# Gated delta rule: key products made on even steps only, odd steps' matrices built by GpSimd from kept copies

## What is computed

```python
decay = jnp.where(tri, jnp.exp(jnp.where(tri, gc[..., :, None] - gc[..., None, :], 0.0)), 0.0)
kb = k * beta[..., None]
lmat = jnp.where(strict, jnp.einsum('bhncd,bhnsd->bhncs', kb, k) * decay, 0.0)
tmat = lax.linalg.triangular_solve(eye + lmat, eye, left_side=True, lower=True)
a_qk = jnp.einsum('bhncd,bhnsd->bhncs', q, k) * decay
...
def step(s, inp):
    v_new = uu - ww @ s
    o = qd @ s + aa @ v_new
    s = s * jnp.exp(gl)[..., None, None] + jnp.einsum('bhcd,bhce->bhde', kd, v_new)
    return s, o
```

## Time and profile before

| | us |
|---|---|
| median of three runs | 2649.49 |
| lowest, highest | 2646.41, 2654.41 |
| the profiled execution, its time | 2650.06 |
| the profiled execution, its span | 2647.9 |
| the scan's eight rounds within it | 921.33 to 1077.47 |

### The profile page before, as it was taken

One profiled execution on the slowest core, in us unless ns is written; L12 is line 12 of the kernel. 1 busy time (PEld: TensorE's weight loads), 2 busy tenths in 40 slices (PEclk: granted clock), 3 DMA queues, 4 the chain that ended last, 5 costly groups with the idle time before them and its releaser, 6 DMA issues.

```text
span 2647.9 us, 43653 instructions
## 1 busy us (share of the span) xinstructions
PE 2502.6 (95%) x15985; PEld 2049.3 (77%) x15985; DVE 1164.5 (44%) x2120; ACT 752.8 (28%) x1539; POOL 1586.7 (60%) x1567
## 2 busy tenths in 40 slices
PE   6999999999999799999999999878999999989997
PEld 4767788887688699778888757866788887678997
DVE  2384511223469787542122330364422223575455
ACT  2263311111541444231111123252311101363332
POOL 2545577775557222557777555685577775655664
PEclk8999999999999899999999999899999999999999
DMA  7355332244523000333334442103323344502552
GB/s 249 101 171 173 115 109 98 96 159 159 177 65 96 32 2 2 116 123 99 100 101 157 161 162 90 55 1 110 129 96 99 101 156 168 196 28 96 184 176 100
DMA packets 217162, 305.07 MB, mean 115 GB/s; under 512 B 7331, under 2 KB 155550, under 8 KB 217023
## 3 DMA queue, kind: packets, MB, share of 16 engines
q1 hardware_dynamic: 190095, 249.66, 28.6%
q10 hardware_dynamic: 26928, 53.48, 5.7%
HBM read 302.07 MB, written 1.05 MB: 114 GB/s over the span
## 4 chain that ended last, share of the span: by engine, by line
PE 80%; DVE 11%; ACT 2%; POOL 2%; issue 2%; DMA 1%; SPq 1%; DVEq 0%; POOLq 0%; ACTq 0%; PEldq 0%
PE bank L1226 42%; PE bank L1945 12%; PE bank L1277 3%; PE bank L1241 2%; PE bank L1976 2%; PE bank L1724 2%; PE bank L1261 2%; PE bank L1774 1%; PE bank L1768 1%; PE bank L1356 1%; PE bank L1332 1%; DVE ztmp L2214 1%; DVE ast L2141 1%; POOL cqf L726 1%; PE bank L1246 1%
## 5 line engine op out<-in xcount | busy, mean ns | idle before, releaser
L657 POOL TENSOR_TENSOR w_lo<-w_raw,w_hi 128x512 fp32r<-128x512 f32 x652 | 858.2, 1316 | 93.7 <-POOL w_hi L654 72.0
L654 POOL TENSOR_SCALAR w_hi<-w_raw 128x512 fp32r<-128x512 f32 x652 | 429.0, 658 | 616.2 <-PE bank L1226 387.0
L1226 PE MATMUL bank<-u_lo,w_hi 128*128 128x512 f32 (+1 forms) x2048 | 759.2, 371 | 9.0 <-DVE u_lo L2062 5.9
L1226 PE MATMUL bank<-u_hi,w_hi 128*128 128x512 f32 (+1 forms) x2048 | 752.0, 367 | 0.0
L1226 PE MATMUL bank<-u_hi,w_lo 128*128 128x512 f32 (+1 forms) x2048 | 751.9, 367 | 0.0
L1226 PEld LDWEIGHTS bank<-u_lo,w_hi 128*128 128x128 f32 x2048 | 389.5, 190 | 88.8 <-issue 18.6
L1226 PEld LDWEIGHTS bank<-u_hi,w_hi 128*128 128x128 f32 x2048 | 389.1, 190 | 63.2
L1226 PEld LDWEIGHTS bank<-u_hi,w_lo 128*128 128x128 f32 x2048 | 389.6, 190 | 61.6
L1945 PE MATMUL bank<-gs_lo,w_hi 128*128 128x512 f32 (+1 forms) x576 | 209.2, 363 | 2.2 <-POOL w_lo L657 2.2
L2748 DVE TENSOR_TENSOR gs_lo<-g,gs_hi 128x512 fp32r<-128x512 f32 (+1 forms) x88 | 108.2, 1240 | 230.2 <-ACT gs_hi L1173 230.2
L1945 PE MATMUL bank<-gs_hi,w_lo 128*128 128x512 f32 (+1 forms) x576 | 208.8, 363 | 0.0
(11 more groups left out here) (350 smaller groups left out, 3757.4 us busy)
## 6 DMA issues: line engine op xcount, KB each, us to landing
w_raw<-in_ffn_w_up SPq DMA_DIRECT2D x88, 1024.0 KB, 5.1
w_raw<-in_ffn_w_down SPq DMA_DIRECT2D x44, 1024.0 KB, 4.9
ada_area<-in_ada_w ACTq DMA_DIRECT2D x39, 1024.0 KB, 15.4
ada_w<-in_ada_w SPq DMA_DIRECT2D x28, 1024.0 KB, 5.2
w_raw<-in_gdn_w_in SPq DMA_DIRECT2D x16, 1024.0 KB, 5.8
w_raw<-in_attn_w_qkv SPq DMA_DIRECT2D x12, 1024.0 KB, 7.9
ada_w<-in_ada_w ACTq DMA_DIRECT2D x12, 1024.0 KB, 6.7
w_raw<-in_gla_w_in SPq DMA_DIRECT2D x12, 1024.0 KB, 5.4
```

Of the source, the lines that this page charges most:

```text
L654: eng.tensor_scalar(w_hi[:, q, :], src, 1.0, 0.0, ALU.mult, ALU.add).then_inc(pool.own, pool.step())
L657: eng.tensor_tensor(w_lo[:, q, :], src, w_hi[:, q, :].bitcast(F32), ALU.subtract).then_inc(w_split, 1)
L1226: mm = eng.matmul(bank[banks[m]][:, T], w[:, q, c:c + P], v[:, k, T], start=(k == 0 and n == 0), stop=(k == KT - 1 and n == 2))
```

## The change

On even steps the key-key and key-query products are made as before and used as before. In addition ScalarE copies them out of PSUM into two new tiles: the key-key products, each head's scaled by the negated beta of the other direction's column, into `bkk`, and the key-query products into `bkq`. On odd steps TensorE makes neither; GpSimd makes NL as D times `bkk` of the other direction, and multiplies AT by `bkq` of the other direction after the masks and the decayed queries. VectorE makes NL and AT on even steps only. On even steps TensorE's 32x32 blocks into banks 3d+1 and 3d+2 wait also for the copies (`kp_ready`). On odd steps VectorE's residual values wait for the masks (`pat_ready`), since they overwrite D, and the outputs wait for AT (`at_ready`). The diff below shows first the tiles, then the code of GpSimd, ScalarE, TensorE and VectorE.

```diff
+        bkk = sb("bkk", [P, 2, 2, 4, P], at=WH0)
+        bkq = sb("bkq", [P, 2, 2, 4, P], at=WH0 + 4 * K4)
+        kept = lambda s, hg: 4 * (s // 2 * 2 + hg)
...
+                        for d in range(2 if s % 2 else 0):
+                            Dm, NLm = bt[d][0], bt[d][3]
+                            eng.wait_ge(dt_ready, pool.next(dt_ready))
+                            eng.wait_ge(kp_ready, kept(s, hg) + 4)
+                            eng.tensor_tensor(NLm[:], Dm[:], bkk[:, hg, 1 - d], ALU.mult).then_inc(nl_ready, 1)
                         for d in range(2):
                             Dm, AT = bt[d][0], bt[d][2]
-                            eng.wait_ge(dt_ready, pool.next(dt_ready))
+                            if s % 2 == 0:
+                                eng.wait_ge(dt_ready, pool.next(dt_ready))
                             eng.tensor_tensor(AT[:], Dm[:], wide(tri[d]), ALU.mult).then_inc(pat_ready, 1)
...
+                        for d in range(2 if s % 2 else 0):
+                            AT = bt[d][2]
+                            eng.wait_ge(pat_ready, 2 * (2 * s + hg) + d + 1)
+                            eng.tensor_tensor(AT[:], AT[:], bkq[:, hg, 1 - d], ALU.mult).then_inc(at_ready, 1)
...
+                        for d in range(2 if s % 2 == 0 else 0):
+                            eng.wait_ge(nl_ready, 2 * (2 * s + hg) + d + 1)
+                            for b in range(4):
+                                c = (1 - d) * B_HEADS + hg * 4 + b
+                                ins = eng.activation(bkk[:, hg, d, b, :], bank[3 * d + 1][:, b * P:(b + 1) * P], ACT.Copy,
+                                                     scale=b_nbeta[:, (s, s ^ 1)[d], c:c + 1])
+                            ins.then_inc(kp_ready, 1)
...
                             ins.then_inc(am_ready, 1)
+                            if s % 2 == 0:
+                                eng.wait_ge(at_ready, 2 * (2 * s + hg) + d + 1)
+                                eng.activation(bkq[:, hg, d], quad(bank[3 * d + 2][:]), ACT.Copy).then_inc(kp_ready, 1)
...
-                        for d in range(2):
+                        for d in range(2 if s % 2 == 0 else 0):
                             for b in range(4):
                                 mm = eng.matmul(bank[3 * d + 1][:, C(b)], bk[:, H(b), tok[d]], bk[:, H(b), tok[d]], start=True, stop=True)
...
+                            if s % 2 == 0:
+                                for b in range(4):
+                                    mm = eng.matmul(bank[3 * d + 2][:, C(b)], bk[:, H(b), tok[d]], bq[:, H(b), tok[d]], start=True, stop=True)
+                                mm.then_inc(kq_ready, 1)
...
-                            eng.wait_ge(at_ready, pe.next(at_ready))
+                            if s % 2 == 0:
+                                eng.wait_ge(at_ready, pe.next(at_ready))
+                                eng.wait_ge(kp_ready, kept(s, hg) + 3 + d)
...
                             eng.wait_ge(qd_ready, pe.next(qd_ready))
+                            if s % 2:
+                                eng.wait_ge(at_ready, pe.next(at_ready))
...
-                        for d in range(2):
+                        for d in range(2 if s % 2 == 0 else 0):
                             Dm, NLm = bt[d][0], bt[d][3]
...
-                        for d in range(2):
+                        for d in range(2 if s % 2 == 0 else 0):
                             AT = bt[d][2]
...
                                 eng.wait_ge(nl_ready, dve.next(nl_ready, 2))
+                                if s % 2:
+                                    dve.skip(dt_ready, 2)
+                                    eng.wait_ge(pat_ready, dve.next(pat_ready, 2))
```

More of the change, by code:

```diff
@@ L401, in build @@
         kq_ready = sem("query_products_ready")
+        kp_ready = sem("products_kept_for_other_direction")
         at_ready = sem("attention_ready")
@@ L1622, in delta_net @@
                                 eng.wait_ge(st_upd, pe.next(st_upd))
-                            for b in range(4):
-                                mm = eng.matmul(bank[3 * d + 2][:, C(b)], bk[:, H(b), tok[d]], bq[:, H(b), tok[d]], start=True, stop=True)
-                            mm.then_inc(kq_ready, 1)
+                            if s % 2 == 0:
+                                for b in range(4):
+                                    mm = eng.matmul(bank[3 * d + 2][:, C(b)], bk[:, H(b), tok[d]], bq[:, H(b), tok[d]], start=True, stop=True)
+                                mm.then_inc(kq_ready, 1)
                         def key_state(d):
```

## The result

The changed kernel takes 2660.65 us (median of ten runs, 2652.88 to 2666.55); the kernel before, run beside it, 2649.14 us (ten runs, 2646.41 to 2654.41). The ratio is 1.0038, with a 95% interval of 1.0028 to 1.0048: some 10 us slower, outside the range of 2642 to 2656. A second set of seven runs, in a later session (e11), gave 1.0039 (1.0023 to 1.0055), so this is the size of it. The profiled execution took 2652.88 us, with a span of 2651.1: it is the shortest of the ten, and shows less of the loss than the usual run does.

A forecast was written before the change was run, and what follows sets the result against it. TensorE's queue was taken to bound the first 8 us of a round. Even rounds' loss less odd rounds' gain, 4 x 1.03 - 4 x 1.23 = -0.8 us, gave 2649.3 us on the profile, 2648.7 on the median; range 2642 to 2656.

The forecast's parts named there:

- The even rounds' loss: Rounds (one step, half the heads) of even steps: TensorE waits for ScalarE's copies, 1.03 us each, 4.1 in four.
- The odd rounds' gain: Rounds of odd steps: products removed, TensorE waits for GpSimd's NL; gain 1.23 us each, 4.9 in four, not 3.58 each.
- The covers: Odd rounds: waits for masks (1.3 us to spare) and for AT (2 us or more) were costed at nothing.
- (c): In odd rounds GpSimd's products slow to 2.2 us beside VectorE and become the bound: +12 us, 2661.5; chance 0.06.
- (a): In even rounds ScalarE's copies cost their upper bound, 2.1 us a round: sum +3.5 us, 2653.0; chance 0.14.
- direction 1's half: Direction 1's part of TensorE's level-a products in odd rounds, run after its NL: 0.39 of 0.78 us.
- the handover: In odd rounds, from the end of GpSimd's NL to TensorE's waiting matmul: 0.14 us.
- Rival (b): Odd rounds gain TensorE's removed 3.58 us whole and the even rounds' copies hide: -14.3 us, 2635.2; chance 0.06.
- rival (d): TensorE's clock falls in the odd rounds' holes, 5 us a fall, +20 us in four rounds, 2668.7; chance 0.04.
- the bounds of two terms: Even rounds' loss between 0.7 and 2.1 us a round, which puts the whole sum at -2.1 to +3.5 us.

The follow-up runs named there:

- e11: Changed kernel unchanged, run again in a later session for a second profile; 2660.25 us against 2648.99, ratio 1.0039.
- e2: Changed kernel with the kept-product tiles filled once by memset, without copies on even steps or waits for them; 2654.6 us against 2647.98, ratio 1.0019.
- e4: Kernel before without the odd steps' products; VectorE makes NL and AT at once from what the banks hold; 2657.14 us against 2647.98, ratio 1.0037.
- e6: Changed kernel with the key-query copies on VectorE behind its AT products, TensorE waiting for the scaled copies alone; 2649.51 us against 2647.2, ratio 1.0012.
- e10: e7 with three unused products instead of eight, all ahead of direction 0's level-a products; 2649.76 us against 2646.62, ratio 1.0007.
- e5: Changed kernel with unused products on odd steps, six ahead of direction 0's level-a products and two ahead of direction 1's; 2654.16 us against 2647.2, ratio 1.0023.
- e7: Changed kernel with the edits of e5 and e6 together; 2643.08 us against 2647.2, ratio 0.9982.
- e8: e7 with direction 1's NL made by VectorE on odd steps and only six unused products; 2641.75 us against 2647.2, ratio 0.9979.
- e9: e5 with direction 1's keys-times-state products moved ahead of its 32x32 products on even steps; 2649.95 us against 2646.62, ratio 1.0010.
- e1: Kernel before with only ScalarE's copies on even steps and TensorE's waits for them added; 2659.26 us against 2647.98, ratio 1.0047.
- e3: Changed kernel with sixteen unused products on odd steps where the removed products stood; 2657.77 us against 2647.98, ratio 1.0036.
- e12: e1's kernel unchanged, run again for a second profile; 2660.6 us against 2648.99, ratio 1.0042.

## Why the prediction was wrong

**What held.** The even rounds' loss: 1.03 us forecast, 1.03 measured. The odd rounds' gain: 1.23 us forecast, 1.10 measured, with TensorE idle for 1.61 + 0.40 us instead of about 1.5 + 0.8. Of the 3.58 us removed go 2.01 for the idling and 0.46 because the halves of L1670, parted by the wait, take 0.62 us each instead of 0.78 together: 1.11 are left. The covers held: no AT or mask was waited for, GpSimd's NL products lasted 1.266 us in the middle and 1.270 at most, so (c) has no support, nor has (a). That the gain came so near is in part luck: direction 1's half was taken at 0.39 us and lasts 0.62, and the handover, taken at 0.14 us, took 0.05. The local sum is 4 x 1.03 - 4 x 1.10 = -0.3 us against a forecast of -0.8. Rival (b) is out: the gain was never 3.58.

**The step that failed is the chance of rival (d),** "TensorE's clock falls in the holes". Its price for one fall was near: 5 us, where the longer falls cost 3.4 to 4.9, since a fall lasts up to 13.7 us and not ten but costs 0.3 to 0.4 us for each and not 0.5. Its +20 us took one such fall in every odd round; the profiles have falls in 12 of 20 rounds with the hole open, some of them short. The forecast put this term at nothing; its chance, 0.04, rested on one window of the earlier trace rows, 776 to 780, with TensorE busy for 2.06 of 4 us at 1.00. That was read as proof that idling for half of such a stretch is harmless. In the changed kernel 984 to 988 is busy for more, 2.54 of 4 us, and the clock falls in it; and round three, with the same hole, keeps 1.00. A busy share and one window that kept the clock were no evidence on how often a hole of two microseconds loses it. The Trainium skill (TensorE: Matmul & The Clock Gate, What's actually happening) says that the activity monitor's window runs freely, so that the same kernel reaches the upper level after a different number of matmuls from run to run; it says so of a kernel's start. No run here shows the window, but the traces agree that the place varies: round three keeps 1.00 and round four falls in the first profile of the changed kernel (0.72), and rounds one, two and three fall in the second (0.73, 0.80, 0.84).

**A second step was missing.** (d) spoke of the odd rounds alone. The even rounds' waits of 0.41 and 0.60 us stand ahead of the two directions' groups of 32x32 products, and the clock falls behind them too. The profiles together, by kind of round:

| rounds | profiles | below 1.00 |
|---|---|---|
| odd, holes open | after, e2, e4, e6, e11 | 12 of 20 |
| odd, three fillers | e10 | 2 of 4 |
| odd, six or eight fillers | e5, e7, e8, e9 | 3 of 16, all at 0.90 |
| odd, products or sixteen fillers | before, e1, e3, e12 | 3 of 16, all at 0.91 |
| even, both waits | after, e1, e3, e5, e11, e12 | 5 of 24 |
| even, one wait | e9 | 0 of 4 |
| even, no wait | before, e2, e4, e6, e7, e8, e10 | 0 of 28 |

The six rounds at 0.90 or 0.91 are all in step 3, and their short dip has another hole: TensorE stands 0.79 us for VectorE's copy of 64x64 blocks there, and the clock falls in that hole or right behind it, in e1's round seven so:
```profile
1055.56 3.04 PE L1705 MATMUL bank<-bD,bTT 128*128 128x128 f32 x16 [0.79 <-DVE bTT L2458]
```
The kernel before has the same wait in the same place, in rounds seven and eight, and keeps 1.00 in its profile; its round eight:
```profile
1070.93 2.02 PE L1689 MATMUL bank<-bD,bTT 128*128 128x128 f32 x16 [0.79 <-DVE bTT L2442]
```
Behind the hole ahead of the level-a products, once it is filled with six products or more, no profile shows a fall: 0 of 16.

From this the missing term can be sized. In after, e2, e6 and e11 the odd rounds lost 4.88 + 16.7 + 6.2 + 2.4 = 30.2 us in 16 rounds against the same round at 1.00 (e4 has no round three at 1.00 to compare with): 1.9 each, 7.6 in four. The even rounds lost 3.0 + 2.0 + 4.4 + 3.8 + 4.0 = 17.2 us in 24: 0.7 each, 2.9 in four. The sum for the change is then -0.3 + 7.6 + 2.9 = +10.2 us; measured were +11.5 and +11.3. For the others: e6 +3.2 against +2.3, e7 -3.9 against -4.1, e3 +8.5 (with 1.5 for round seven's dip) against +9.8; but e1 +8.5 against +11.3 and +11.6, e2 +3.2 against +6.6, e5 +3.1 against +7.0. The shares are an estimate from few rounds, and partly from the very profiles that they are set against.

The clocks of all the runs, and not of one profile each, close most of this gap. Take the waits alone from the rounds at 1.00, and for the falls 1900 us for each unit by which the median of a kernel's mean clocks lies below 0.980 (us, medians, against the kernel before; e8's and e9's short dips in step 3 are taken out of the waits at 1.5 us each):

| kernel | clock | waits | clock's part | sum | measured |
|---|---|---|---|---|---|
| changed | 0.9725 | -0.3 | +14.2 | +13.9 | +11.5 |
| e11, the same | 0.974 | -0.3 | +11.4 | +11.1 | +11.3 |
| e1, e12 | 0.976 | +4.1 | +7.6 | +11.7 | +11.3, +11.6 |
| e2 | 0.974 | -4.4 | +11.4 | +7.0 | +6.6 |
| e3 | 0.977 | +4.1 | +5.7 | +9.8 | +9.8 |
| e5 | 0.977 | +0.2 | +5.7 | +5.9 | +7.0 |
| e6 | 0.976 | -4.4 | +7.6 | +3.2 | +2.3 |
| e7 | 0.980 | -3.9 | 0 | -3.9 | -4.1 |
| e8 | 0.979 | -7.2 | +1.9 | -5.3 | -5.5 |
| e9 | 0.978 | +0.5 | +3.8 | +4.3 | +3.3 |
| e10 | 0.976 | -4.4 | +7.6 | +3.2 | +3.1 |

A clock is on record to 0.001, which is 1.9 us, and over the runs of every kernel taken together (199) the slope is 1700 and not 1900 us; within that, waits and lost clock are the whole of the change in every kernel of the table (e4, without a round three at 1.00, is left out). The table doesn't say where in a kernel the clock was lost; that it was lost behind the scan's holes is shown by e2 and e1, which open one kind each, and by e7, which closes both and has the clock and the gain back.

**The range** took in the scatter of three runs and the bounds of two terms, but no term for the clock, whose price alone (up to +20 us) was over five times the larger bound of the sum (+3.5).

**What stays open.** The halves do not add: +11.3 for the even one and +6.6 for the odd one, and +11.5 for both. The waits do add; the lost clock doesn't (0.004 with the even holes, 0.006 with the odd ones, 0.006 to 0.0075 with both), and why is not shown. Why all five falls in even rounds are in rounds one and two (ahead of round one the clock is low for part of the time in every profile, 0.54 from 914.50 to 922.00 in the changed kernel's first; whether that bears on it was not tried). Why the short dip comes in round seven of e1, e3 and e12 (19.24 us at 0.91), and in neither of the kernel before's step 3 rounds, which have the same 0.79 us wait. What exactly TensorE has to be doing to keep the clock was not found: three fillers did not do, six or eight did. And a single profile tells little of a kernel whose clock falls by chance: e12's stood 17.2 us above the profile of before, of which the scan has 164.6 - 155.2 = 9.4; the rest is in unchanged code.

## What to carry to other kernels

When a change takes work from an engine that is the bound, ask first what fills the time until its next input; on TensorE a hole of two microseconds here cost more by the clock than the removed work gave. Give such a risk its own term, its price times how often it may strike in all the rounds, and do not let one window that kept the clock settle it. Where the input cannot come sooner, unused products in the hole (e7) kept the gain; sharing the work between engines (e8) shortened rounds three and four by another 0.86 us each, though its median is only 1.3 us lower, within the scatter. One profile is not enough for a kernel whose clock falls by chance: the mean clocks of all its runs said what single profiles missed.

## What the runs showed of the hardware

- The granted clock fell to 0.50 behind holes of 1.6 + 0.4 us (odd rounds), of 0.41 + 0.60 us ahead of 32x32 products (even rounds) and of 0.79 us (step 3), in some executions and rounds and not in others; a fall lasted up to 13.7 us, and the longer ones cost 0.3 to 0.4 us for each of them (0.36 in round four).
- Eight unused 128x128 products of 0.22 us each in the odd rounds' hole kept the clock up behind it in twelve rounds of twelve (e5, e7, e9; the one dip there, to 0.90, is at the 0.79 us hole of round eight); with three it fell in two of four.
- VectorE and GpSimd with two SBUF inputs each wait for each other: in the four odd rounds of e8 L2450 starts 0.18 to 0.27 us before GpSimd's NL product ends and is done 0.54 to 0.56 us after that end, and the first mask behind it takes 1.72 us in round three instead of 1.27. The Trainium skill (SBUF — State Buffer, Who interferes with whom) has one of them shut out while the other runs, and the trace agrees, with GpSimd's 0.45 us lost.
- ScalarE's 128x128 copies from PSUM with a pointer scale take 0.368 us each and follow at 0.26 us.
